# A two-layer hybrid decoder on one core: one fused mask-and-minimum pass in attention, remainders moved to GpSimd, and a new order of work around three norms

## The reference

```
h     = rmsnorm(x) * g_mix                     # mean of squares over 1024, then 1/sqrt
mixed = [gated linear attention | gated recurrence | dilated softmax attention](h @ w_in)
x     = x + mixed @ w_out
h     = rmsnorm(x) * g_ffn
x     = x + swiglu(h)                          # layer 0: one block, width 2816
x     = x + top-2 of 8 swiglu experts(h)       # layer 1
```

## Time and profile before

| what | us |
|---|---|
| median of 3 runs (2077.15 to 2086.19) | 2078.82 |
| the profiled execution | 2080.65 |
| its span, first to last instruction | 2078.5 |
| PE busy | 1936.1 (93%) |
| DVE busy | 1036.6 (50%) |
| ACT busy | 828.8 (40%) |
| POOL busy | 266.5 (13%) |

### The profile page before, as it was taken

One profiled execution on the slowest core, in us unless ns is written; L12 is line 12 of the kernel. 1 busy time (PEld: TensorE's weight loads), 2 busy tenths in 40 slices (PEclk: granted clock), 3 DMA queues, 4 the chain that ended last, 5 costly groups with the idle time before them and its releaser, 6 DMA issues.

```text
span 2078.5 us, 37745 instructions
## 1 busy us (share of the span) xinstructions
PE 1936.1 (93%) x15803; PEld 1706.0 (82%) x15803; DVE 1036.6 (50%) x1355; ACT 828.8 (40%) x1193; POOL 266.5 (13%) x328
## 2 busy tenths in 40 slices
PE   7999788989999999989999789889889999999997
PEld 5999677669999999988899777669767777777775
DVE  5245564663433233324234564673346666667664
ACT  4344322552322122222344322462235666656564
POOL 2000552000100000002000443200300110011100
PEclk9999878999999999999999988999979999999998
DMA  5551201954663466311452200982447877778874
GB/s 186 185 176 64 97 1 41 413 239 158 236 242 102 143 239 242 105 59 51 162 193 106 97 2 3 365 325 86 159 162 252 287 269 277 288 261 285 284 265 119
DMA packets 79950, 375.55 MB, mean 181 GB/s; under 512 B 10160, under 2 KB 10576, under 8 KB 72496
## 3 DMA queue, kind: packets, MB, share of 16 engines
q1 hardware_dynamic: 72528, 354.47, 46.7%
q0 software_dynamic: 7296, 19.23, 3.2%
HBM read 357.21 MB, written 84.37 MB: 212 GB/s over the span
## 4 chain that ended last, share of the span: by engine, by line
PE 80%; DVE 9%; ACT 4%; issue 3%; DMA 2%; POOL 2%; POOLq 0%; SPq 0%; ACTq 0%; DVEq 0%
PE ps L1274 36%; PE ps L1752 17%; PE ps L1759 6%; PE ps L1324 5%; PE ps L1290 4%; PE ps L1268 2%; PE ps L1389 2%; DVE expert_weights_lo L2310 1%; ACT expert_weights_hi L1194 1%; PE ps L1423 1%; DMA normed_or_mixed<-s_hgrn 1%; DVE small L2113 1%; PE ps L1571 1%; DVE scratch L2110 1%; ACT scratch L1056 1%
## 5 line engine op out<-in xcount | busy, mean ns | idle before, releaser
L2310 DVE TENSOR_TENSOR expert_weights_lo<-weight_ring,expert_weights_hi 128x1408 fp32r<-128x1408 f32 (+1 forms) x141 | 203.3, 1475 | 102.2 <-ACT expert_weights_hi L1194 101.7
L1194 ACT ACTIVATE expert_weights_hi<-weight_ring 128x1408 fp32r<-128x1408 f32 (+1 forms) x144 | 178.2, 1262 | 99.5 <-PE ps L1752 99.5
L1274 PE MATMUL ps<-ffn_in_hi,weights_hi 128*128 128x288 f32 x704 | 208.7, 296 | 3.3 <-DVE weights_lo L2185 3.3
L1274 PE MATMUL ps<-ffn_in_lo,weights_hi 128*128 128x288 f32 x704 | 207.7, 295 | 0.0
L1274 PE MATMUL ps<-ffn_in_hi,weights_lo 128*128 128x288 f32 x704 | 207.0, 294 | 0.0
L1274 PE MATMUL ps<-proj_in_hi,proj_weights_hi 128*128 128x288 f32 x608 | 183.8, 302 | 0.0
L1752 PE MATMUL ps<-expert_weights_hi,item_in_hi 128*128 128x352 f32 x512 | 172.8, 338 | 9.1 <-DVE expert_weights_lo L2310 5.4
L1274 PE MATMUL ps<-proj_in_lo,proj_weights_hi 128*128 128x288 f32 x608 | 179.3, 295 | 0.0
L1274 PE MATMUL ps<-proj_in_hi,proj_weights_lo 128*128 128x288 f32 x608 | 178.7, 294 | 0.0
L1752 PE MATMUL ps<-expert_weights_hi,item_in_lo 128*128 128x352 f32 x512 | 167.2, 327 | 0.0
L1752 PE MATMUL ps<-expert_weights_lo,item_in_hi 128*128 128x352 f32 x512 | 166.9, 326 | 0.0
(11 more groups left out here) (351 smaller groups left out, 4399.4 us busy)
## 6 DMA issues: line engine op xcount, KB each, us to landing
weight_ring<-w_gu_moe SPq DMA_DIRECT2D x89, 704.0 KB, 7.0
ok_s<-kcache SPq DMA_DIRECT2D x16, 2032.0 KB, 10.3
ov_s<-vcache SPq DMA_DIRECT2D x16, 2032.0 KB, 10.1
weight_ring<-w_dn_moe SPq DMA_DIRECT2D x55, 512.0 KB, 5.7
residual<-w_gu_moe SPq DMA_DIRECT2D x39, 704.0 KB, 6.5
weight_ring<-w_gu SPq DMA_DIRECT2D x44, 512.0 KB, 4.8
weight_ring<-w_feat SPq DMA_DIRECT2D x38, 512.0 KB, 3.7
residual<-w_dn_moe SPq DMA_DIRECT2D x33, 512.0 KB, 4.3
```

Of the source, the lines that this page charges most:

```text
L1194: nc.scalar.activation(EWh[:, j % NW, 0:w], slot[:, 0:w], ACT.Copy).then_inc(ew_hi, 1)
L1274: op = nc.tensor.matmul(out, x, y, start=k == 0 and n == 0, stop=k == kn - 1 and n == 2)
L2310: v.tensor_tensor(EWl[:, j % NW, 0:w], slots[q][:, 0:w], EWh[:, j % NW, 0:w], ALU.subtract).then_inc(ew_split, 1)
```

## The change

- *Mask and maximum in one pass.* The two masks are multiplied by sqrt(64) on the host. One `tensor_tensor_reduce` computes (score + mask) x (-1/8) and its minimum along the row; a prompt step needs one for each of its two heads. For a sample the minimum starts from `new_negmax`, the minimum over its new keys, computed once a layer. Scores thus stand negated in SBUF, and the exponential has scale -1. The semaphores `sc_free` and `ssc_free` go (their declarations are left out below); PE waits for `mx_ready`.
- *Remainders of the mixed output* go from DVE to POOL, behind POOL's wait for its stores.
- *`OUT_ORDER`* becomes 0 to 7. With 6 ring slots, the loads of output weights 6 and 7 wait for the slots of units 0 and 1.
- *`shift`* stands behind odd units, from j = 3 on, instead of even ones from j = 0.
- *Norms.* `norm` calls a hook behind the squares. Layer 0's second norm rounds two weights there and the third behind the root; DVE takes the third remainder behind chunk 1. Layer 1's first norm rounds its first weight behind the squares, and DVE takes its remainder before it waits for the root. In layer 0's first norm two DVE instructions change places.
- *Squares at the end of the feed-forward block.* Those of chunks 1 to 5 are added at m = 6, and that of chunk 6 at m = 7.

```diff
 assert U_EXP % NSPLIT == 0
-OUT_ORDER = (2, 3, 4, 5, 0, 1, 6, 7)
+OUT_ORDER = tuple(range(8))
...
 u = np.arange(SEQ)[None, :]
-c["lnc"] = log_mult(SEQ - P + p - u, SEQ - P + p - u >= 0)
+c["lnc"] = log_mult(SEQ - P + p - u, SEQ - P + p - u >= 0) * np.float32(DH ** 0.5)
 d = PAST + t - np.arange(PAST)[None, :]
-c["smask"] = np.where(live, log_mult(d, d >= 0), 0).astype(np.float32)
+c["smask"] = np.where(live, log_mult(d, d >= 0), 0).astype(np.float32) * np.float32(DH ** 0.5)
...
 Os = [V[:, 1 + b // 4, b % 4 * P:b % 4 * P + P] for b in range(NB)]
+new_negmax = SM[:, 8:16]
...
 sp.dma_start(ring[:, s, 0:1024], src).then_inc(w_land[s], 16)
-if j % 2 == 0 and j < 20:
-    shift(e * 5 + (3 + j // 4), (j // 2) % 2)
+if j % 2 == 1:
+    late = (j - 3) // 2
+    if 0 <= late < 10:
+        shift(e * 5 + (3 + late // 2), late % 2)
...
 pool.wait_ge(stored_s, (L + 1) * 64)
+for n, k in enumerate(SPLIT_ORDER):
+    pool.wait_ge(mixhi_ready, 9 * L + n + 1)
+    w = T if k < 4 else SEQ
+    nc.gpsimd.tensor_tensor(Ml[:, k, 0:w], mix[:, k, 0:w], Mh[:, k, 0:w], ALU.subtract).then_inc(mixlo_ready, 1)
+pool.wait_ge(mixhi_ready, 9 * (L + 1))
+nc.gpsimd.tensor_tensor(Ml[:, 4:8, SEQ:T], mix[:, 4:8, SEQ:T], Mh[:, 4:8, SEQ:T], ALU.subtract).then_inc(mixlo_ready, 1)
...
-def norm(k, buf, out, wait_x, between=lambda c: None, first=0):
+def norm(k, buf, out, wait_x, first=0, behind_squares=lambda: None):
     for c in range(first, KC):
-        between(c)
         square(k, buf, c)
+    behind_squares()
...
-hi(0)
+if L:
+    norm(2 * L, sq, rinv, wait_mix, 0, lambda: hi(0))
+else:
+    norm(2 * L, sq, rinv, wait_mix)
+    hi(0)
...
 for h in range(2):
-    op = nc.scalar.activation(Pp[i][:, h, :], Pp[i][:, h, :], ACT.Exp, bias=negmax[:, 2 * i + h:2 * i + h + 1],
+    op = nc.scalar.activation(Pp[i][:, h, :], Pp[i][:, h, :], ACT.Exp, bias=negmax[:, 2 * i + h:2 * i + h + 1], scale=-1.0,
...
 act.wait_ge(smx_ready, n + 1)
-nc.scalar.activation(Ps, Ps, ACT.Exp, bias=s_negmax[:, b % 2:b % 2 + 1],
+nc.scalar.activation(Ps, Ps, ACT.Exp, bias=s_negmax[:, b % 2:b % 2 + 1], scale=-1.0,
...
-def first_weights(c, L=L):
-    for j in {KC - 2: (0,), KC - 1: range(1, NSPLIT)}.get(c, ()) if L == 0 else ():
+def first_weights(L=L):
+    for j in range(NSPLIT - 1) if L == 0 else ():
-norm(2 * L + 1, sqf, rinv_f, lambda c: act.wait_ge(out_evac, PF0[L] + c + 1), first_weights, KC - 2)
+norm(2 * L + 1, sqf, rinv_f, lambda c: act.wait_ge(out_evac, PF0[L] + c + 1), KC - 2, first_weights)
 if L == 0:
+    hi(0, NSPLIT - 1)
...
 if n >= 1:
-    pe.wait_ge(sc_free, n0 + n)
+    pe.wait_ge(mx_ready, n0 + n)
...
     lower_bound_inputs()
+else:
+    lo(0)
...
                        ALU.mult, ALU.mult).then_inc(pf_ready, 1)
-if c in (1, 3):
-    lo(c // 2)
     v.tensor_tensor(Pl[:, 0, :], sq[:, 0, :], Ph[:, 0, :], ALU.subtract).then_inc(h_odd, 1)
+    if L == 0:
+        lo(0)
+if c == 3:
+    lo(1)
...
     dve.wait_ge(pt_ps, n0 + n - TT + 1)
-mask = const["lnc"][:, SEQ - w:SEQ].rearrange("p (o s) -> p o s", o=1).to_broadcast([P, 2, w])
-v.scalar_tensor_tensor(Pp[i], ps[:, 0:2, 0:w], DH ** -0.5, mask, ALU.mult, ALU.add).then_inc(sc_free, 1)
-dve.wait_ge(sc_free, n0 + n + 1)
-v.tensor_reduce(negmax[:, 2 * i:2 * i + 2], Pp[i], AX.X, ALU.max, negate=True).then_inc(mx_ready, 1)
+mask = const["lnc"][:, SEQ - w:SEQ]
+for h in range(2):
+    op = v.tensor_tensor_reduce(Pp[i][:, h, :], ps[:, h, 0:w], mask, -DH ** -0.5, 3e38, ALU.add, ALU.min,
+                                negmax[:, 2 * i + h:2 * i + h + 1])
+op.then_inc(mx_ready, 1)
...
 dve.wait_ge(ssc_done, n + 1)
-v.scalar_tensor_tensor(Ps[:, 0:PAST], ps[:, 4:6, :].rearrange("p a t -> p (a t)"), DH ** -0.5,
-                       const["smask"], ALU.mult, ALU.add).then_inc(ssc_free, 1)
-dve.wait_ge(ssc_free, n + 1)
-v.tensor_reduce(s_negmax[:, b % 2:b % 2 + 1], Ps, AX.X, ALU.max, negate=True).then_inc(smx_ready, 1)
+v.tensor_tensor_reduce(Ps[:, 0:PAST], ps[:, 4:6, :].rearrange("p a t -> p (a t)"), const["smask"], -DH ** -0.5,
+                       new_negmax[:, b:b + 1], ALU.add, ALU.min, s_negmax[:, b % 2:b % 2 + 1]).then_inc(smx_ready, 1)
...
 dve.wait_ge(new_done, L + 1)
-link(v.scalar_tensor_tensor(new_scores, ps[:, 4, :], DH ** -0.5, const["smask_new"], ALU.mult, ALU.add))
+link(v.scalar_tensor_tensor(new_scores, ps[:, 4, :], -DH ** -0.5, const["smask_new"], ALU.mult, ALU.subtract))
+link(v.tensor_reduce(new_negmax, new_scores.rearrange("p (b s) -> p b s", b=NB), AX.X, ALU.min))
...
     prompt_normed(2 * c)
-for k in SPLIT_AT.get(c, ()):
-    dve.wait_ge(mixhi_ready, 9 * L + SPLIT_ORDER.index(k) + 1)
-    w = T if k < 4 else SEQ
-    v.tensor_tensor(Ml[:, k, 0:w], mix[:, k, 0:w], Mh[:, k, 0:w], ALU.subtract).then_inc(mixlo_ready, 1)
...
-dve.wait_ge(mixhi_ready, 9 * (L + 1))
-v.tensor_tensor(Ml[:, 4:8, SEQ:T], mix[:, 4:8, SEQ:T], Mh[:, 4:8, SEQ:T], ALU.subtract).then_inc(mixlo_ready, 1)
...
-for j in range(NSPLIT):
+for j in range(NSPLIT - 1):
...
                        ALU.mult, ALU.mult).then_inc(hf_ready, 1)
+if c == 1:
+    lo(0, NSPLIT - 1)
...
 v.tensor_tensor(split(X[:, m, :]), split(X[:, m, :]), pair(j % 4), ALU.add).then_inc(out_evac, 1)
-if e == EXPERTS[0] - 1 and m >= 2:
-    add_square(2, sq, m - 1)
+if e == EXPERTS[0] - 1 and m >= KC - 2:
+    for c in range(1, KC - 2) if m == KC - 2 else (KC - 2,):
+        add_square(2, sq, c)
```

More of the change, by code:

```diff
@@ L426, in build @@
             "o_done", "osq_ready", "oss_done", "orinv_ready", "mixl_ready"))
-        sc_done, sc_free, mx_ready, p_ready, pn_ready, pt_ps, pt_ready, pv_done, mixc_ready = (sem(n) for n in (
-            "sc_done", "sc_free", "mx_ready", "p_ready", "pn_ready", "pt_ps", "pt_ready", "pv_done", "mixc_ready"))
+        sc_done, mx_ready, p_ready, pn_ready, pt_ps, pt_ready, pv_done, mixc_ready = (sem(n) for n in (
+            "sc_done", "mx_ready", "p_ready", "pn_ready", "pt_ps", "pt_ready", "pv_done", "mixc_ready"))
         qs_ready, spv_half, os_ready, os_turned = (sem(n) for n in ("qs_ready", "spv_half", "sample_out_ready", "sample_out_turned"))
-        ssc_done, ssc_free, smx_ready, sp_ready, spt_ps, spt_ready, spv_done, smix_ready = (sem(n) for n in (
-            "ssc_done", "ssc_free", "smx_ready", "sp_ready", "spt_ps", "spt_ready", "spv_done", "smix_ready"))
+        ssc_done, smx_ready, sp_ready, spt_ps, spt_ready, spv_done, smix_ready = (sem(n) for n in (
+            "ssc_done", "smx_ready", "sp_ready", "spt_ps", "spt_ready", "spv_done", "smix_ready"))
         sig_ready = sem("sig_ready")
@@ L910, in wait_mix @@
                         act.wait_ge(out_evac, pf_ffn(0) + KC + c + 1)
-                norm(2 * L, sq, rinv, wait_mix)
                 def hi(u, L=L):
```

## The result

The changed kernel takes 2049.47 us (median of 4 runs, 2045.42 to 2055.34) against 2078.16 us before: ratio 0.9856, 95% interval 0.9837 to 0.9875. The forecast was 2053, range 2044 to 2067. On another chip the ratio was 0.9879 (0.9862 to 0.9896). The profiled execution, the slowest of the four, took 2055.34 us, its span 2053.6; that is 25.3 us less than the one before, where the sum of the prediction said 25.7.

A forecast was written before the change was run, and what follows sets the result against it. PE was four fifths of the last chain, so only its stands or lower clock could go, with attention floored by the cache's landing. Terms of 25.7 us off 2080.65 gave 2055.0, or 2053 as median; range 2044 to 2067.

The forecast's parts named there:

- the sum: All predicted gains added: 6.4 + 6.0 + 2.6 + 8.5 + 2.2 = 25.7 us off the profiled 2080.65 us.
- attention: Attention stage of each layer: 6.4 us gained in layer 0, 6.0 in layer 1.
- layer 1's start: PE's wait for the first remainder of layer 1's normed input goes: 2.2 us gained, bounds 0.9 and 3.9.
- the tail: From the end of the last scores to the first output product, 13.5 us: 2.6 gained, less 1.0 for blocking.
- It can only remove what the work lags behind it: In attention, faster DVE cannot beat the cache's landing; it removes only lags of 4.3 us (layer 0) and 3.9 (layer 1).
- second value pieces are used within some 0.5 us of landing: Sign for the forecast in attention: second value pieces of samples 1 to 6 used within some 0.5 us of landing.
- The fused pass: Mask and maximum in attention: 1.4 us a sample instead of 2.5, 1.7 us for the widest prompt step instead of 2.44.
- the rival of several times that price: Slower case, chance 0.06: the fused instruction takes several times the time per element; at 4 times, 2105 us.
- The move to POOL: Mixed remainders leave DVE in attention, with its 8.9 us of waits for ACT; blocking costs 0 to 2.2 us a layer, 1.0 taken.
- The wait at the last normalisation: Sign against the forecast, at the end of attention: wrong if a wait appears at the last normalisation.
- Both steps: Feed-forward block: layer 0's start gains 2.6 us by earlier weights and squares; the end gains 8.5 us by later square additions.
- Layer 0's first norm: Two DVE instructions change places in layer 0's first norm: no change beyond 0.6 us either way.

The follow-up runs named there:

- The parts alone: The kernel before with one part each: squares 2070.51 us; natural order, shifts, first feed-forward weights 2077.89; fused pass 2062.70; remainders on POOL 2071.95; first norms 2080.80.

## Why the prediction was right, and where not

- *The sum* came within 1 us (25.7 forecast, 25.3 between the profiled executions), but not by its terms alone: attention gave 2.3 us less and layer 1's start 1.6 more, and 1.0 and 1.5 lost and 2.0 gained stand at places that the sum has at nothing. That these cancel is luck.
- *Attention.* 12.4 us were forecast, 10.1 measured. Up to the end of the last prompt scores it gained 4.7 and 4.3 us, of 4.8 and 4.4 in the sum; the tail behind gave 1.2 a layer, of 1.6, and layer 0 lost 1.5 to the clock. "It can only remove what the work lags behind it" held: the lag of 4.3 us on sample 6 went to nothing, and PE then waits for the cache (that second value pieces are used within some 0.5 us of landing holds in layer 0 from sample 4 on, and not for samples 1 to 3). What was read wrongly is where the lag came from. With the DMA full I took the cache for the pace of the kernel before; with half the bytes it ran no faster. Its own chain, scores to mask to maximum to exponential to turn, made it 10.05 us a sample, PE standing 6.1 us a layer in it, and the cache at full rate happens to need as long. The row that tells this, PE's waits by line over the stage, was not read; one of its seven waits (0.52) entered the sum. Without a floor by the cache the gain would have been nearly the same, as PE was full. So the size fits by luck: PE's own pace, 9.4 us, lies just under that of the cache.
- *The fused pass* has the price of the nearest row, as chosen; the 0.15 us an instruction for the delivery of the minimum is not there (1.29 and 1.31 us, not 1.4 and 1.7), and the rival of several times that price is out.
- *The move to POOL.* Blocking was forecast at "From 0 to 2.2 us a layer; I take 1.0"; it came as 1.07 us on the output weight, 1.0 on the last normalisation, and in one of two executions 1.5 of lower clock. The remainders themselves were cheaper than the earlier trace rows, 1.42 us at 576 columns for the first of them, and PE never waited on one: the 1.88 was read where DVE worked beside POOL, and the step from 0.76 on DVE is a factor of 1.9, not 2.5. The wait at the last normalisation, named as a sign against the forecast, is 1.1 us and was 1.7 before. What failed is the credit given to the move, 1.8 us of the tail less 1.0: DVE's waits for ACT, 8.9 us in the earlier trace rows, were no one's wait once the pass was fused, and the move then costs 0.5 us a layer.
- *Feed-forward block.* Both steps came as worked out (2.6 and 8.5; 2.7 and 8.8), and alone as well.
- *Layer 1's start* came out at the upper bound, 3.8 of 3.9 us: the low clock went with the wait.
- *Layer 0's first norm* is the step whose mechanism failed: "no change beyond 0.6 either way". PE started 1.1 us sooner, but the third weight's remainder stood behind the lower bounds in DVE's order and did not move; the stand there grew from 0.8 to 3.6 us, and the clock fell behind it. The net loss was 1.8 and 3.4 us at 60 us in the two executions.

The parts alone gain 8.0, 0.6, 15.8 and 6.6 us, and the norms nothing: 31 in all, against 25 to 29 together. The move to POOL, 6.6 us alone and nothing beside the fused pass, accounts for the difference, within what these runs can tell.

## What to carry to other kernels

A full DMA queue does not prove that it sets the pace: read what the busiest engine waits for, summed by line over the stage, and halve the bytes where both come out alike. Two edits that shorten the same wait do not add up; here the second brought only its side effects. Starting an engine sooner pays only if the next thing that it needs is not fixed elsewhere; if it is, the stand grows and may cost the clock as well.

## What the runs showed of the hardware

- The fused pass, with scores in PSUM and a mask in SBUF, was not slowed beside POOL: at 434.23 it took 1.28 us while a remainder ran on POOL from 434.37, for 1.41. In all eight such overlaps of that execution the pass took 1.28 us. The normalisation, with one operand in SBUF, went from 0.88 to 1.90 us for two. The Trainium skill (SBUF — State Buffer, section Who interferes with whom) names both cases, one SBUF input outside the 2-port modes and `tensor_scalar` within them; the trace agrees.
- The clock behind a stand is not the same in each execution of one kernel, nor in both layers of one. In the changed kernel, behind the same 2.5 us ahead of the output projection, it was 0.62 in layer 0 of one execution, and 1.00 in its layer 1 and in both layers of the other; behind the 2.0 us between the halves of the feed-forward block it was 0.83 in one execution and 1.00 in the other. After the 3.6 us at 38 us it fell in each of the five executions that have that stand.
